# Moving three conv taps within the lockstep of a hybrid RWKV and conformer step

## What is computed

```python
def conformer_branch(u, buf0, lp):
    u = u + lp["glu_b"]
    val, gate = jnp.split(u, 2, axis=-1)
    glu = val * jax.nn.sigmoid(gate)
    xpad = jnp.concatenate([buf0.astype(glu.dtype), glu], axis=1)
    y = lax.conv_general_dilated(xpad, lp["conv_w"][:, None, :].astype(xpad.dtype),
                                 window_strides=(1,), padding="VALID",
                                 dimension_numbers=("NWC", "WIO", "NWC"),
                                 feature_group_count=C_CONV) + lp["conv_b"]
    y = jax.nn.silu(layer_norm(y, lp["conv_ln_g"], lp["conv_ln_b"]))
    return y @ lp["w_pw"] + lp["b_pw"], xpad[:, -(CONV_WIDTH - 1):]
...
# rwkv, token by token: S_t = S_{t-1} diag(w_t) + (S_{t-1} a_t) b_t^T + v_t k_t^T ;  y_t = S_t r_t
```

## Time and profile before

| | us |
|---|---|
| median of 3 runs | 1056.23 (1055.63 to 1056.33) |
| profiled execution | 1057.64 |
| its span, first to last instruction | 1055.9 |
| TensorE busy | 1034.8 (98%) |
| VectorE busy | 682.7 (65%) |
| ScalarE busy | 517.8 (49%) |
| GpSimd busy | 356.4 (34%) |

### The profile page before, as it was taken

One profiled execution on the slowest core, in us unless ns is written; L12 is line 12 of the kernel. 1 busy time (PEld: TensorE's weight loads), 2 busy tenths in 40 slices (PEclk: granted clock), 3 DMA queues, 4 the chain that ended last, 5 costly groups with the idle time before them and its releaser, 6 DMA issues.

```text
span 1055.9 us, 25943 instructions
## 1 busy us (share of the span) xinstructions
PE 1034.8 (98%) x10943; PEld 972.5 (92%) x10943; DVE 682.7 (65%) x1216; ACT 517.8 (49%) x967; POOL 356.4 (34%) x194
## 2 busy tenths in 40 slices
PE   8999999999999999999999999999999999999998
PEld 8998898998988998999999768989999999999998
DVE  5488888788785666786570791657998989500004
ACT  6455534544544567525462544654665665522232
POOL 4431221332312310256232101353544544444450
PEclk9999999999999999999999999999999999999999
DMA  7321221220223433655154774523334334433222
GB/s 228 100 70 35 61 62 43 61 76 27 62 62 102 130 102 130 209 180 164 57 200 160 259 276 131 147 76 105 110 92 120 105 97 121 161 115 100 81 64 82
DMA packets 164059, 120.41 MB, mean 114 GB/s; under 512 B 5336, under 2 KB 153066, under 8 KB 163433
## 3 DMA queue, kind: packets, MB, share of 16 engines
q1 hardware_dynamic: 159979, 108.08, 33.0%
q10 hardware_dynamic: 3974, 10.80, 2.9%
HBM read 111.04 MB, written 8.30 MB: 113 GB/s over the span
## 4 chain that ended last, share of the span: by engine, by line
PE 80%; DVE 13%; ACT 3%; DMA 2%; issue 2%; POOL 0%; DVEq 0%; ACTq 0%; SPq 0%
PE ps L556 34%; PE ps L1811 15%; PE ps L538 10%; PE ps L1168 10%; DVE conv_y L2859 5%; PE ps L1878 3%; PE ps L578 2%; DVE cache L3301 1%; DMA q_bc<-q_scratch 1%; PE ps L1115 1%; DVE ps L3214 1%; PE ps L604 0%; DMA w_raw<-in_w_gate_up_dram 0%; DMA x_tok<-in_x_prompt_dram 0%; DVE m_lo L640 0%
## 5 line engine op out<-in xcount | busy, mean ns | idle before, releaser
L1004 POOL TENSOR_TENSOR w_lo<-w_raw,w_hi 128x1024 fp32r<-128x1024 f32 (+2 forms) x83 | 193.7, 2338 | 408.7 <-ACT w_hi L596 356.5
L556 PE MATMUL ps<-h_hi,w_hi 128*128 128x260 f32 x748 | 161.8, 297 | 1.1 <-DVE gate_b L3156 0.5
L556 PE MATMUL ps<-h_hi,w_lo 128*128 128x260 f32 x748 | 150.2, 282 | 0.0
L556 PE MATMUL ps<-h_lo,w_hi 128*128 128x260 f32 x748 | 150.2, 282 | 0.0
L596 ACT ACTIVATE w_hi<-w_raw 128x1024 fp32r<-128x1024 f32 (+2 forms) x95 | 91.2, 965 | 74.0 <-PE ps L556 62.1
L556 PEld LDWEIGHTS ps<-h_hi,w_hi 128*128 128x128 f32 x748 | 115.3, 188 | 10.5 <-issue 4.4
L556 PEld LDWEIGHTS ps<-h_lo,w_hi 128*128 128x128 f32 x748 | 115.2, 188 | 0.0
L556 PEld LDWEIGHTS ps<-h_hi,w_lo 128*128 128x128 f32 x748 | 115.2, 188 | 0.0
L2859 DVE SCALAR_TENSOR_TENSOR conv_y<-glu,prm,conv_y 128x512 f32<-128x512 f32 x120 | 106.6, 889 | 2.5
L3199 DVE TENSOR_TENSOR sq_acc<-sq_acc,sq_tmp 128x264 f32<-128x264 f32 (+2 forms) x35 | 28.6, 816 | 114.8 <-ACT sq_tmp L2718 76.0
L1055 POOL TENSOR_TENSOR w_lo<-w_raw,w_hi 128x512 fp32r<-128x512 f32 x36 | 50.5, 1403 | 98.7 <-ACT w_hi L2601 98.7
(11 more groups left out here) (574 smaller groups left out, 3087.1 us busy)
## 6 DMA issues: line engine op xcount, KB each, us to landing
w_raw<-in_w_gate_up_dram SPq DMA_DIRECT2D x44, 512.0 KB, 4.7
w_raw<-in_w_in_dram SPq DMA_DIRECT2D x38, 512.0 KB, 3.7
cache<-in_cache_mem_k_dram SPq DMA_DIRECT2D x16, 512.0 KB, 6.3
w_raw<-in_w_down_dram SPq DMA_DIRECT2D x16, 512.0 KB, 3.7
cache<-in_cache_mem_v_dram SPq DMA_DIRECT2D x14, 512.0 KB, 7.3
w_raw<-in_w_k_dram SPq DMA_DIRECT2D x8, 512.0 KB, 3.9
w_raw<-in_w_v_dram SPq DMA_DIRECT2D x8, 512.0 KB, 3.6
w_raw<-in_w_out_dram SPq DMA_DIRECT2D x8, 512.0 KB, 3.7
```

Of the source, the lines that this page charges most:

```text
L556: mm = nc.tensor.matmul(ps[:, 2 * s + a, 0:width], w[:, k, :], x[:, x0 + k, a * width:(a + 1) * width], start=(first and k == 0 and n == 0 ...
L1004: pool.tensor_tensor(lo[:, 0:kts], w_raw[:, b % RAW_SLOTS, 0:kts], hi[:, 0:kts].bitcast(F32), ALU.subtract).then_inc(w_lo_ready, 1)
```

## The change

Per pass three taps change their place; their number stays 31 and TAP_LEAD stays as it is. One fewer stands ahead of dbl0 (behind akv's second group in pass 0, behind its first in the others). Behind dbl3's second group stands one in place of two, and one stands behind dbl4's first group, that is between the writes of its two groups. Behind h's first group, at the lockstep's end, stand two in place of one.

```diff
 TAP_LEAD = (2, 4)
-TAP_FILL = ((0, 0, 0, 1, 0, 0) + (3, 3, 2, 2) + (1,) * 7 + (2, 0, 0, 1, 1) + (1, 1, 0, 4, 1, 0),
-            (0,) * 6 + (3, 3, 2, 1) + (1,) * 7 + (2, 0, 0, 1, 1) + (1, 1, 0, 4, 1, 0))
+TAP_FILL = ((0, 0, 0, 1, 0, 0) + (3, 3, 2, 1) + (1,) * 7 + (1, 1, 0, 1, 1) + (1, 1, 0, 4, 2, 0),
+            (0,) * 6 + (3, 3, 1, 1) + (1,) * 7 + (1, 1, 0, 1, 1) + (1, 1, 0, 4, 2, 0))
```

## The result

The changed kernel takes 1066.13 us (median of 5 runs, 1065.14 to 1067.10) against 1056.23 for the kernel before beside it (1055.63 to 1057.83): a ratio of 1.0091, interval 1.0079 to 1.0102. It is slower, as forecast; the forecast was 1063.0 and the range ended at 1066.0. The median lies 0.13 above that end, and the end lies within its noise (by the interval, 1064.6 to 1067.0). The profiled execution took 1065.53 with a span of 1063.6.

A forecast was written before the change was run, and what follows sets the result against it. TensorE, busy 98% of the span, was taken as the bound, so only its waits count. Terms -2.84 + 8.80 + 0.78 = +6.74 us on the profiled 1057.64 gave 1064.4, or 1063.0 against the median; range 1061 to 1066, widened to 1058.5 to 1066.

The forecast's parts named there:

- Ahead of dbl0: One tap fewer before the first doubling shortens TensorE's wait there: 2.84 us gained over four passes.
- The tap at dbl4: Between dbl4's groups the tap stands still until GpSimd's split ends, delaying dbl5: 10.60 us lost, 8.80 after give-back.
- The 0.52 behind dbl5: TensorE's wait for dbl5's second copy, expected to vanish: 0.52 us in one pass, 1.8 in four.
- none would stand for L2883: Sign at dbl5: TensorE's wait of about 2.6 us would be listed under L2061 or L2890, none under L2883.
- Rivals 1 to 3: At dbl4: split waits for tap, 1058.5 (0.05); no tap held, 1055.2 (0.06); TensorE has slack at dbl5, 1052.4 (0.04).
- The end: One tap more at the lockstep's end: nothing lost in passes 0 to 2, 0.78 us at pass 3's window-row load.
- rival 4: Idle TensorE at dbl5 drops to half clock for 2.25 us of work per pass: 9.0 more, 1072; chance 0.05.

The follow-up runs named there:

- e1: Kernel before with one tap per pass moved from ahead of dbl0 to the lockstep's end, none at dbl4: 1053.53 us, ratio 0.9983.
- e4: Changed kernel with 18 surplus matmuls, result unused, between dbl5's two groups to fill TensorE's wait: 1061.95 us, ratio 1.0045 to the kernel before.
- e6: Changed kernel with ScalarE's rounding and GpSimd's split of one weight block six steps later: 1052.32 us, ratio 0.9958 to the kernel before.
- e3: Kernel before with one tap moved from behind dbl3 to the lockstep's end, nothing else: 1057.25 us, ratio 1.0010.
- e5: Changed kernel with one projection slice moved from behind dbl5's second group to behind its first: 1060.89 us, ratio 1.0036 to the kernel before.
- e8: Kernel before with the rounding and split later and one tap moved from ahead of dbl0 to between dbl4's groups: 1051.17 us, ratio 0.9945.
- e2: Kernel before with only one tap moved from behind dbl3 to between dbl4's groups: 1071.18 us, ratio 1.0135.
- e7: Kernel before, its taps unchanged, with ScalarE's rounding and GpSimd's split of one weight block six steps later: 1054.89 us, ratio 0.9978.

## Why the prediction was right, and what it mis-sized

*Ahead of dbl0: right.* -2.84 was forecast, the wait fell from 3.6 to 0.9 (2.7), and e1 shows the gain without the tap at dbl4.

*The tap at dbl4: right in mechanism and size.* It stood still until the split's end and 0.55 more; 2.6 were forecast for it and 2.59 measured; the write behind it was to come 2.65 late and in pass 0 comes at 104.70, where without the tap it would have followed the 101.87 by 0.21 as in the earlier trace rows, that is 2.62 late. The 0.52 behind dbl5 came back. TensorE's wait of about 2.6 is there four times, 10.2 in all against 10.60 forecast. The name was wrong: I wrote that none would stand for L2883, and all of it does, by the profile's inference, in e4 too; e6's loads show that L2883 is not what TensorE waits for. Rivals 1 to 3 are out: the split was not held (2.36), the tap was, and TensorE had no slack. The Trainium skill ("SBUF — State Buffer", Who interferes with whom) states that a VectorE instruction with two SBUF inputs contends with a GpSimd instruction that reads SBUF, that one with at most one such input does not (outside modes that play no part here), and that issue order decides who is held. The trace agrees: a tap asked for 0.3 us behind the split's start takes 2.59, a write from PSUM during the same split (101.87) 0.29, and the same tap without the split beside it 0.74. The Trainium skill ("SBUF — State Buffer", A bandwidth-pool intuition that's wrong) states that descriptor writing locked out by a copy goes on about 0.115 us after the copy's end. A tap does not follow that here: it has already ended 0.55 behind the split, less than its plain 0.74.

*The end: right in kind, and in size by luck.* In passes 0 to 2 nothing was counted, and nothing was lost: the split did get in ahead of the subtraction (L2842), which took 3.69 us in place of 1.75, and TensorE waited for no write of VectorE behind it. In pass 3 TensorE's wait for the window rows went from 0.4 to 1.3 (1.2 forecast). But 0.47 of that is the load, which took longer (4.00 in place of 3.53); that was not forecast. The tap alone is worth about 0.4 of the 0.78 counted: with the same six taps there and loads of 3.36 to 3.42 the waits are 0.7 to 0.8 (e1, e3, e4, e5). e8, with five taps and a load of 4.08, waits 1.1. No run changed the load by itself, so why it takes between 3.36 and 4.08 stays open.

*The clock: the step that was mis-sized.* It stood as rival 4 with a chance of 0.05 and a price of 9.0 on top, because no wait in the trace of before was so long and no row showed half clock. It came in three passes of four. From the second half of dbl5 to the projection slices behind the applying step, TensorE's loads need 5.84 us in pass 0 (105.42 to 111.26), 5.84 in pass 1 and 5.93 in pass 2, and 4.32 in pass 3, at full clock. That is 1.52, 1.52 and 1.61 lost, 4.65 for three, in place of nothing in the forecast and 9.0 in the rival: the rival took 2.25 us of work, and all four passes, to be at half clock; the low clock began behind dbl5, covered work of about 1.6, and spared one pass. e4 gives some 4 by removing the falls.

*What was not in the sum on the other side.* As measured, the terms that the forecast had are -2.7, +8.4 (10.2 less 1.8) and +0.9, together 6.6 against 6.74 forecast; with the clock's 4.65 they give 11.2. By the end of the four passes, TensorE's product of 86 matmuls stands at 355.62 in place of 346.25, 9.37 later, so 1.9 came back that no term names. The chain of the kernel before has four pieces of TensorE's own issue time in passes 1 to 3 (0.64, 0.44, 0.36 and 0.43 us, 1.87 in all), the chain after has two, in pass 2 (0.28 and 0.18); that is 1.4 of the 1.9, read from the chains alone, and no run tried it. The rest is not placed. The medians differ by 9.9; the two profiled executions only by 7.9, since that of before lay 1.41 above its median, that of after 0.60 below its own. From about 600 to 632 us the changed kernel's lag falls from 9.2 to 7.7, where the chain of before has a transfer of 5.80 (at 613.74) that the chain after lacks.

So the forecast of 1063.0 fell short of 1066.13 by the clock, less what came back elsewhere: two things that were not in its sum, of opposite sign. That the time still came out at the end of the range is partly luck.

*What stays open.* Why the clock fell in some passes and not in others. The length of the wait does not decide it alone: the changed kernel's 2.44 in pass 3 was spared and e2's 2.44 in pass 3 was not, and of e5's waits of 1.77 one in three led to a fall. That the wait matters is shown: with it filled (e4) or gone (e6) no pass of the profiled execution has a fall at dbl5.

## What to carry to other kernels

An instruction's price on VectorE is that of the place, not of the instruction: look at what GpSimd runs at that moment and at how many SBUF inputs both have, and reckon the rest of GpSimd's instruction as a hold. When TensorE's wait grows to some us (here 1.8 to 2.6), add the work behind it at half clock as a term of its own, and look for it in narrow windows, since the page's slices hide it. Before moving the held work, try moving the holder, if nobody is waiting for it: here the same move of three taps cost 9.9 us with the split beside dbl4 and won 2.6 with it six steps later (e6 against e7).

## What the runs showed of the hardware that was not expected

In the changed kernel TensorE's waits of 2.60 us were followed by half clock in three passes of three and the one of 2.44 was not, while the 1.28 us of the earlier trace rows left the clock at 1.00 in each us from 89 to 96. The Trainium skill ("TensorE: Matmul & The Clock Gate", What's actually happening) states that TensorE runs at 1.2 GHz when idle or cold and at 2.4 GHz when it has been busy; the trace agrees with the two levels, 0.50 and 1.00 in the rows above. What I had not expected is that the fall can come when TensorE is long at work again: in pass 1 of the changed kernel dbl5's second group starts at 179.57, the granted clock is 1.00 from 180 to 181 and 0.52 from 181 to 182. In the profiled executions of e2, e3, e5 and e6 the clock also fell once near the start (0.50 to 0.58 in the mean from 10 to 12 us), in those of the other kernels it did not, and no edit touches that stretch; so a fall can also differ from one execution to the next, and one profiled execution of each kernel is all that the counts of passes above rest on.
